# Input projection of a transformer block: 64 of 73 weight blocks multiplied in pairs by seven quarter products

## The reference, cut to what matters

```python
def in_proj(h, w_in):
    cuts = np.cumsum(IN_SIZES)[:-1].tolist()
    return jnp.split(h @ w_in, cuts, axis=-1)
```

## Time and profile before

| | |
|---|---|
| Median of 3 runs | 5343.04 us (5340.18 to 5347.0) |
| Profiled execution, own time | 5340.29 us |
| Its span in the trace | 5338.1 us |
| Input projection, first to last matmul | 127.9 to 1008 us |
| TensorE busy, whole span | 96% |
| VectorE busy | 47% (none of it in this stage after the first block) |

### The profile page before, as it was taken

One profiled execution on the slowest core, in us unless ns is written; L12 is line 12 of the kernel. 1 busy time (PEld: TensorE's weight loads), 2 busy tenths in 40 slices (PEclk: granted clock), 3 DMA queues, 4 the chain that ended last, 5 costly groups with the idle time before them and its releaser, 6 DMA issues. The chain is left out here.

```text
span 5338.1 us, 89996 instructions
## 1 busy us (share of the span) xinstructions
PE 5102.9 (96%) x33252; PEld 4964.4 (93%) x33252; DVE 2513.0 (47%) x3845; ACT 848.1 (16%) x1331; POOL 3462.1 (65%) x2044
## 2 busy tenths in 40 slices
PE   7999999999999888989889999999998999999998
PEld 7999999999989776989889999999998999999998
DVE  4000000022111333530207787888885788888866
ACT  4000000033322333100102111121111000000001
POOL 7555555444344233545447777888887799999985
PEclk9999999999999999999999999999999999999999
DMA  7333333432232433652324444888987888888863
GB/s 256 111 111 112 109 109 109 126 108 88 77 125 101 170 129 117 221 178 79 118 104 135 137 135 172 319 321 325 329 329 254 308 309 301 310 308 302 305 215 105
DMA packets 344664, 1011.48 MB, mean 189 GB/s; under 512 B 39681, under 2 KB 133729, under 8 KB 308849
## 3 DMA queue, kind: packets, MB, share of 16 engines
q1 hardware_dynamic: 164960, 524.56, 29.1%
q0 software_dynamic: 36864, 268.45, 13.2%
q10 hardware_dynamic: 142640, 215.86, 11.4%
HBM read 883.11 MB, written 126.76 MB: 189 GB/s over the span
## 5 line engine op out<-in xcount | busy, mean ns | idle before, releaser
L221 POOL TENSOR_TENSOR w_lo<-w_raw,w_hi 128x1024 fp32r<-128x1024 f32 x878 | 2157.8, 2458 | 163.4 <-POOL w_hi L217 160.9
L217 POOL TENSOR_SCALAR w_hi<-w_raw 128x1024 fp32r<-128x1024 f32 x878 | 967.9, 1102 | 1598.6 <-PE ps L254 1353.6
L250 PE MATMUL ps<-h_hi,w_hi 128*128 128x272 f32 (+1 forms) x6816 | 1736.6, 312 | 80.8 <-PEq L1692 15.4
L254 PE MATMUL ps<-h_hi,w_lo 128*128 128x272 f32 (+1 forms) x6816 | 1716.6, 309 | 0.0
L252 PE MATMUL ps<-h_lo,w_hi 128*128 128x272 f32 (+1 forms) x6816 | 1706.6, 308 | 0.0
L250 PEld LDWEIGHTS ps<-h_hi,w_hi 128*128 128x128 f32 x6816 | 1142.6, 189 | 106.4 <-issue 101.5
L252 PEld LDWEIGHTS ps<-h_lo,w_hi 128*128 128x128 f32 x6816 | 1142.3, 190 | 5.9
L254 PEld LDWEIGHTS ps<-h_hi,w_lo 128*128 128x128 f32 x6816 | 1136.1, 190 | 2.8
L250 PE MATMUL ps<-ex_c_hi,w_hi 128*128 128x416 f32 x2048 | 719.8, 351 | 22.5 <-DVE ex_c_lo L2490 22.5
L254 PE MATMUL ps<-ex_c_hi,w_lo 128*128 128x416 f32 x2048 | 724.3, 354 | 0.0
L252 PE MATMUL ps<-ex_c_lo,w_hi 128*128 128x416 f32 x2048 | 716.7, 350 | 0.0
(11 more groups left out here) (273 smaller groups left out, 4778.3 us busy)
## 6 DMA issues: line engine op xcount, KB each, us to landing
w_raw<-weights SPq DMA_DIRECT2D x906, 512.0 KB, 3.3
up<-up_out ACTq DMA_DIRECT2D x128, 208.0 KB, 2.9
gate<-g_sb_g ACTq DMA_DIRECT2D x13, 2048.0 KB
ex_up<-up ACTq DMA_DIRECT2D x32, 832.0 KB
ex_gate<-gate ACTq DMA_DIRECT2D x32, 832.0 KB
proj<-in_stage ACTq DMA_DIRECT2D x73, 272.0 KB, 2.1
br_gate<-proj ACTq DMA_DIRECT2D x48, 272.0 KB, 3.7
mem_x_part<-x ACTq DMA_DIRECT2D x8, 1088.0 KB, 6.5
```

What stands on the lines that cost most here:

```text
L217: pool.tensor_scalar(self.whi[:, slot, :], self.raw[:, slot, :], 1.0, 1.0, ALU.mult, ALU.mult).then_inc(self.hi_done, 1)
L221: pool.tensor_tensor(self.wlo[:, slot, :], self.raw[:, slot, :], self.whi[:, slot, :].bitcast(F32), ALU.subtract).then_inc(self.split_done, 1)
L250: pe.matmul(acc, hi, x, start=first, stop=False)
L254: mm = pe.matmul(acc, lo, x, start=False, stop=last)
```

## The change

The nine first blocks (`SINGLE`) stay as they were, but with two accumulators instead of four. The other 64 make 32 pairs. For a pair, the weights are a 2x2 matrix of pieces (two blocks by two halves of the 2048 features: a11, a12, a21, a22) and the activations one of 2x2 quarters (two feature halves by two token halves). Winograd's form of Strassen's algorithm makes the four output quarters from seven products of a piece with a quarter, in place of eight. Each product is 8 chunks x 3 matmuls of 272 columns in one PSUM bank (`product`), banks 0 to 6.

- Four sums of activations per chunk (`sum_operand`, VectorE, with the hi part by ScalarE in `round_operand`) are made once, during the first singles.
- Per pair: four weight sums of 128x1024 (s1 to s4) and seven lo parts on VectorE, seven hi parts on ScalarE. GpSimd splits nothing between `AT_PAIRS` and `AT_LATER`; then it waits for both counters and splits the four pieces of the next stage.
- Per pair: ScalarE copies product 3 into `in_stage`; VectorE adds the others in seven additions of 128x272 (`result`), from a PSUM bank and `in_stage`; ScalarE applies the sigmoid (last two pairs) and stores.
- TensorE waits before each product for its weights' lo part, and from the second pair on for its bank (the result that last read it, or the copy). The pairs run as four unrolled and then a loop of seven turns of four. VectorE and ScalarE are written out in full.
- The host swaps the two blocks of each pair in memory, so that a21 and a22 come first.

Elsewhere three semaphores are merged into others, with the same waits (`gain_loaded` into `x_loaded[0]`, `squares_summed` and `tokens_turned` into one); and `Norm` creates two semaphores fewer where they are not used. The core of the diff:

```diff
+class Winograd:
...
+    PRODUCTS = ("s3", "s1", "a22", "a11", "s2", "a12", "s4")
+    RAW = ("a21", "a22", "a11", "a12")
+    SUMS = {"s1": 0, "s2": 0, "s4": 0, "s3": 1}
+    FREES = ("s1", "lo_a22", "lo_a11", "lo_a12")
+    ROUNDED_RAW = ("a22", "a11", "a12", "s4")
+    STEPS = ("s3", "lo_s3", "lo_s1", "s2", "lo_s2", "s4", "lo_s4")
+    RESULTS = ("u2", "u3", "u4", "c22", "c21", "c11", "c12")
+    OPERAND_STEPS = 7
+    TURN = 4
...
+    def sum_operand(self, dve, k):
+        first, rest = slice(0, HALF), slice(HALF, T)
+        x = [self.sums[:, half, 0:T] for half in range(2)]
+        t = [self.t_sums[:, i, :] for i in range(4)]
+        if k:
+            dve.wait_ge(*self.did_operand(self.OPERAND_STEPS, k - 1))
+        for half in range(2):
+            at = PIECE_K * half + k
+            dve.tensor_tensor(x[half], self.hi[:, at, :].bitcast(F32), self.lo[:, at, :].bitcast(F32),
+                              ALU.add).then_inc(self.steps, 1)
+        dve.wait_ge(*self.did_operand(2, k))
+        dve.tensor_tensor(t[0], x[0][:, rest], x[0][:, first], ALU.subtract).then_inc(self.steps, 1)
+        dve.tensor_tensor(t[2], x[1][:, rest], x[0][:, rest], ALU.subtract).then_inc(self.steps, 1)
+        dve.wait_ge(*self.did_operand(3, k))
+        dve.tensor_tensor(t[1], x[1][:, rest], t[0], ALU.subtract).then_inc(self.steps, 1)
+        dve.wait_ge(*self.did_operand(5, k))
+        dve.tensor_tensor(t[3], x[1][:, first], t[1], ALU.subtract).then_inc(self.steps, 1)
+        dve.wait_ge(self.rounded, k + 1)
+        dve.tensor_tensor(self.t_lo[:, k, :, :], self.t_sums, self.t_hi[:, k, :, :].bitcast(F32),
+                          ALU.subtract).then_inc(self.steps, 1)
+    def round_operand(self, act, k):
+        act.wait_ge(*self.did_operand(6, k))
+        act.activation(self.t_hi[:, k, :, :], self.t_sums, ACT.Copy).then_inc(self.rounded, 1)
...
+    def round_weights(self, act, p, n):
+        name, g = self.PRODUCTS[p], 7 * n + p
+        if g < RING:
+            act.wait_ge(self.core.piece_used, self.at - RING + g + 1)
+        else:
+            act.wait_ge(*self.did_product((g - RING) % 7, (g - RING) // 7))
+        if g < RING:
+            act.wait_ge(self.core.hi_done, self.at)
+        if name in self.SUMS:
+            act.wait_ge(*self.did_weights(name, n))
+        else:
+            self.wait_raw(act, name, n)
+        act.activation(self.core.whi[:, self.slot(p, n), :], self.source(name), ACT.Copy
+                       ).then_inc(self.did_round(p, n)[0], 1)
...
+    def sum_weights(self, dve, name, n):
+        needs, last_use, a, op, b = {
+            "s3": (("a21", "a11"), ("lo_s3", n - 1), "a11", ALU.subtract, "a21"),
+            "s1": (("a21", "a22"), ("lo_s4", n - 1), "a21", ALU.add, "a22"),
+            "s2": (("a11",), ("lo_s1", n), "s1", ALU.subtract, "a11"),
+            "s4": (("a12",), ("lo_s2", n), "a12", ALU.subtract, "s2")}[name]
+        for raw in needs:
+            self.wait_raw(dve, raw, n)
+        if last_use[1] >= 0:
+            dve.wait_ge(*self.did_weights(*last_use))
+        else:
+            dve.wait_ge(*self.did_operand(self.OPERAND_STEPS, PIECE_K - 1))
+            dve.wait_ge(self.core.split_done, self.at)
+        dve.tensor_tensor(self.source(name), self.source(a), self.source(b), op
+                          ).then_inc(self.did_weights(name, n)[0], 1)
+    def rest_of_weights(self, dve, p, n):
+        name, slot = self.PRODUCTS[p], self.slot(p, n)
+        dve.wait_ge(*self.did_round(p, n))
+        dve.tensor_tensor(self.core.wlo[:, slot, :], self.source(name), self.core.whi[:, slot, :].bitcast(F32),
+                          ALU.subtract).then_inc(self.did_weights(f"lo_{name}", n)[0], 1)
...
+    def product(self, pe, p, slot, n, free):
+        if needed(n):
+            pe.wait_ge(*(self.did_result(free, n - 1) if free else (self.copied, n)))
+        pe.wait_ge(*self.did_weights(f"lo_{self.PRODUCTS[p]}", n))
+        held(pe)
+        out = self.core.ps[:, p, 0:HALF]
+        x_hi, x_lo = self.operand(p, self.hi, self.t_hi), self.operand(p, self.lo, self.t_lo)
+        for k in range(PIECE_K):
+            hi = self.core.whi[:, slot, k * P:(k + 1) * P]
+            lo = self.core.wlo[:, slot, k * P:(k + 1) * P]
+            pe.matmul(out, hi, x_hi(k), start=k == 0, stop=False)
+            pe.matmul(out, hi, x_lo(k), start=False, stop=False)
+            mm = pe.matmul(out, lo, x_hi(k), start=False, stop=k == PIECE_K - 1)
+        mm.then_inc(self.did_product(p, n)[0], 1)
+    def products(self, pe, n_pairs):
+        free = ("u3", "c22", "c21", None, "u2", "c11", "c12")
+        pe.wait_ge(*self.did_operand(self.OPERAND_STEPS, PIECE_K - 1))
+        def body(q):
+            for u in range(self.TURN):
+                for p in range(7):
+                    self.product(pe, p, self.slot(p, u), self.TURN * q + u, free[p])
+        rounds(pe, n_pairs // self.TURN, body)
...
+    def result(self, dve, name, n, stored):
+        first, rest = slice(0, HALF), slice(HALF, T)
+        m0, m1 = 2 * (n % 2), 2 * (n % 2) + 1
+        part = lambda m, t: self.stage[:, m, t]
+        bank = lambda p: self.core.ps[:, p, 0:HALF]
+        to, a, p, after = {
+            "u2": (part(m0, rest), part(m0, first), 4, None), "u3": (part(m1, first), part(m0, rest), 0, "u2"),
+            "u4": (part(m0, rest), part(m0, rest), 1, "u3"), "c22": (part(m1, rest), part(m1, first), 1, "u3"),
+            "c21": (part(m1, first), part(m1, first), 2, "c22"), "c11": (part(m0, first), part(m0, first), 5, "u2"),
+            "c12": (part(m0, rest), part(m0, rest), 6, "u4")}[name]
+        if name == "u2":
+            dve.wait_ge(self.copied, n + 1)
+        if name == "u3":
+            dve.wait_ge(*stored)
+        if after:
+            dve.wait_ge(*self.did_result(after, n))
+        if name in ("u2", "c11", "c12"):
+            dve.wait_ge(*self.did_product(p, n))
+        dve.tensor_tensor(to, a, bank(p), ALU.add).then_inc(self.added, 1)
...
+    def vector(self, dve, n_pairs, stored):
+        for n in range(n_pairs + 1):
+            results = lambda *names: [self.result(dve, name, n - 1, stored(n - 1)) for name in names] if n else None
+            if n < n_pairs:
+                self.sum_weights(dve, "s3", n)
+                self.sum_weights(dve, "s1", n)
+                self.rest_of_weights(dve, 0, n)
+                self.rest_of_weights(dve, 1, n)
+            results("u2", "u3", "u4", "c22", "c21")
+            if n < n_pairs:
+                self.rest_of_weights(dve, 2, n)
+            results("c11")
+            if n < n_pairs:
+                self.sum_weights(dve, "s2", n)
+                self.rest_of_weights(dve, 3, n)
+            results("c12")
+            if n < n_pairs:
+                self.rest_of_weights(dve, 4, n)
+                self.sum_weights(dve, "s4", n)
+                self.rest_of_weights(dve, 5, n)
+                self.rest_of_weights(dve, 6, n)
+    def copy_product(self, act, n, stored):
+        act.wait_ge(*stored)
+        act.wait_ge(*self.did_product(3, n))
+        act.activation(self.stage[:, 2 * (n % 2), 0:HALF], self.core.ps[:, 3, 0:HALF], ACT.Copy
+                       ).then_inc(self.copied, 1)
...
 def stage_input_projection(core, hi, lo, kv_stored):
     nc, io = core.nc, core.io
+    PAIRS = (IN_BLOCKS - LATER - SINGLE) // 2
+    GATE_PAIR = (B_GATE - SINGLE) // 2
+    AT_PAIRS = AT_IN + 2 * SINGLE
     with ExitStack() as ctx:
...
-        plain, gates = (B_GATE - 1) // 4, (IN_BLOCKS - LATER - B_GATE) // 4
+        stored_singles = lambda u: len(range(u, SINGLE, 4))
+        stored_by = lambda m, n: (stored[2 * (n % 2) + m], 16 * (stored_singles(2 * (n % 2) + m) + n // 2))
         @block.sync
         def _(sp):
...
         def _(pool):
-            core.split_pieces(pool, AT_IN + RING, AT_LATER + RING)
-        def one_block(pe, b, u, in_round):
-            if needed(b - 3):
-                pe.wait_ge(out_ready, b - 3)
-            held(pe)
-            for piece in range(2):
-                core.use_piece(pe, (AT_IN + 2 * in_round + piece) % RING, 2 * b + (AT_IN + piece), [
-                    (core.acc(u), parts(hi, k), parts(lo, k), k == 0, k == KD - 1)
-                    for k in range(PIECE_K * piece, PIECE_K * (piece + 1))])
+            core.split_pieces(pool, AT_IN + RING, AT_PAIRS)
+            pool.wait_ge(core.hi_done, AT_LATER)
+            pool.wait_ge(core.split_done, AT_LATER)
+            core.split_pieces(pool, AT_LATER, AT_LATER + RING)
         @block.tensor
         def _(pe):
-            one_block(pe, 0, 3, 0)
-            def body(q):
-                for u in range(4):
-                    one_block(pe, 4 * q + (u + 1), u, u + 1)
-            rounds(pe, plain + gates, body)
+            for b in range(SINGLE):
+                if b >= 2:
+                    pe.wait_ge(out_ready, b - 1)
+                for piece in range(2):
+                    i = AT_IN + 2 * b + piece
```

(113 more changed lines are left out.)

25 lines of the change are left out of this document (13 added, 12 removed).

## The result

The changed kernel takes 5249.14 us (median of 4 runs, 5241.81 to 5256.26) against 5341.61 before: ratio 0.9826, interval 0.9809 to 0.9843. The forecast was 5248. Run again later, its median of five was 5246.46, ratio 0.9831 (0.9815 to 0.9848).

A forecast was written before the change was run, and what follows sets the result against it. TensorE's matmuls were taken to bound the stage. 5340.3 - 96.2 (fewer matmuls) + 0.9 (entry) + 1.6 (exit) = 5246.6 us, or 5249.3 in the median's terms; 5248 was taken, range 5240 to 5285.

The forecast's parts named there:

- part 1: Input projection's pairs: 168 matmuls instead of 192 at 125.3 ns each, saving 96.2 us over 32 pairs.
- part 2: VectorE's new work in the pairs: 16.5 of 21.05 us, 78%, hidden behind TensorE at no cost.
- The plan of the period: Order of one pair's steps from product 3's end: no late TensorE wait, smallest margin 2.7 us at product 0 for u3.
- parts 3 and 4: Transitions into and out of the pairs: 0.9 us added at the entry and 1.6 us at the exit.
- Entry: Into the pairs: TensorE waits 0.9 us for the last single's evacuation, bounds 0.6 and 3.
- Activation sums: During the first singles: 45 us for eight chunks, twice that if GpSimd's splits interfere, of 108; hidden.
- Exit: Stage's end: TensorE gap 5.9 us, 1.6 more than before, because GpSimd splits the next stage's four pieces late.
- part 5: Instruction supply for the pairs' longer loop body, 672 matmuls and 7 turns: costs 0, at most 10 us.
- The first: Rival: TensorE waits once a pair for u3's bank, 1 to 2 us each, 5280 to 5312 us; chance 0.12.
- The second: Rival: VectorE bounds the pairs, 2.69 us a step beside GpSimd, 277 us more, 5617 us; chance 0.04.
- The third: Rival: no saving, products cost as much as the halves did, about 5343 us; chance 0.02.

The follow-up runs named there:

- E1: Changed kernel with an eighth product, 24 more matmuls into an unread bank, in each pair: 5338.81 us, ratio to before 0.9999.
- E8: The changed kernel run again unaltered, for a second trace: 5246.46 us (5 runs).
- E2: Changed kernel with idle VectorE steps in each pair: three ahead of u2 5240.35 us, five there 5287.55, five behind the last lo part 5248.35.
- E3: Changed kernel with GpSimd doing two unread 128x512 subtractions behind each of products 3 to 6 of every pair: 5294.21 us, ratio 0.9916.

## Why the prediction was right

**The matmuls (part 1).** Forecast 96.2 us. From the first product's start (242.71) to the last matmul's (917.23) are 5375 steps of 125.5 ns, against 125.3 taken: 1.0 us dearer over the stage. One bank for 24 matmuls in a row costs no more than that, and whether the bank is the cause was not tried. The estimate by the Trainium skill's formula for a matmul (VectorE: DVE Perf Modes, section on the TRN2 errata), 116 ns and a saving of 89 us, does not agree with this trace: 125.5 ns, and E1 measured 96.8 us for the 768 matmuls.

**VectorE's work (part 2).** Steps of 1.22 and 0.43 us as worked out. Its share is 75%, not 78%: the start of one step lies some 0.08 us before the end of the step ahead in the trace (two 1024-column sums take 2.35 us, not 2.44). The plan of the period held. In the trace, with product 3's end at about 507.9, lo of s3 ends at 2.9 (3.0 forecast), u3 at 6.3 (6.3), and product 0 starts at 8.9 (9.0). TensorE waited for no result in 32 pairs.

**The seams (parts 3 and 4).** Entry 0.9 forecast. The gap is 0.86, but from the last single's last matmul to the first product's are 1.15 us where a step is 0.125, and the next step is 0.08 longer: 1.1 us in all. Activation sums 45 to 90 us forecast, 47.8 measured (131.2 to 179.0): GpSimd's splits lengthened the first addition of six chunks by 0.2 to 1.4 us, no more. That the first product starts at 242.7 and not at the 239 forecast is the late start of the whole stage in this trace (131.3 against 127.9); in E8's it starts at 239.9. Exit 5.9 forecast, 6.02 measured, and by the engine named. Of all terms this one was easiest to miss: it stands nowhere near the sevenths saved, but follows from two rows and the question what each engine must still do before the barrier.

**Instruction supply (part 5).** Nothing forecast, nothing seen: no gap of TensorE between the entry and the exit.

**The sum.** The stage's length fell from 884.3 us (127.87 to 1012.19) to 792.2 (131.34 to 923.54), by 92.1 where 96.2 - 0.9 - 1.6 = 93.7 was forecast; 1.0 of the difference is the step of the matmul, 0.2 the entry, 0.1 the exit, the rest the stage's first block. The medians fell by 92.5. The traced execution fell by only 84 us, as it drew long stretches elsewhere (E8): one trace of each kernel would have put 8 us on the change that don't belong to it. That the forecast came within 1.1 us of the median (5248 against 5249.14) is in part luck: the same kernel's median was 5246.46 the second time, and that of the kernel before lay between 5334.15 and 5342.62 in the four sets of its runs. What the stage shows is a sum within 1.6 us, with each of its terms near its size.

**The rivals.** The first (a wait a pair for u3) is real, but needs more work ahead of u2 than there is, somewhere above the 2.1 us that cost nothing and under the 3.5 that cost 40 (E2). The second (VectorE as the bound) takes GpSimd's help. E3 made it true with a mean of 1.81 us over the eleven steps, between the 1.63 from which the rival had the gain shrink and the 1.90 at which it had it gone: 43 us over the changed kernel, and still faster than before. Its 277 us, counted over the kernel before, were for 2.69 us in every step. The third (no saving) fell with E1.

## What to carry to other kernels

Where TensorE is busy all the time and VectorE and ScalarE are not, an algorithm with fewer products pays its full eighth of matmuls, if the order of the additions is laid out against the ends of the products and the smallest margin is known by name; here it was 2.6 us of 21. Five more steps, 3.5 us, right ahead of that result cost 40 us; the same steps 6 us earlier in the round cost nothing in the pairs, as VectorE's own waiting took up 1.3 us of them, with 0.35 us to spare. Work that an engine used to do ahead of a barrier comes back as a wait if its inputs now come late: leave the last of it for behind the barrier. And take the gain from the stage that was changed, in two traces if there are two, before explaining anything outside it.

## What the runs showed of the hardware

A wait of TensorE that is met in time costs nothing, and one that is met late costs more than its lateness: 1.25 us for a result 0.9 us late (E2), 2.1 for one 1.8 late (E3). GpSimd beside VectorE lengthened only the steps with two SBUF inputs (1.22 to means between 1.70 and 2.05 us), and GpSimd's own steps of 128x512 took 2.01 us in the mean there, 1.3 with none of these beside them; steps with one PSUM input stayed at 0.43. Behind each barrier that ended with GpSimd's split, TensorE started 0.5 us after the split's end. Matmuls of 272 columns step at 125.3 ns when two accumulators alternate and at 125.5 ns in the products, each into one bank; what makes the 0.2 ns was not tried.
